# Gate tiles projected one ahead of the branch tiles, in an attention and mixture-of-experts step on one core

## The reference, cut to what matters

```python
g_da, g_mla, g_swa = jnp.split(jax.nn.sigmoid(h @ p['w_gate']), 3, axis=-1)
merged = (g_da * (o_da @ p['w_br_da']) + g_mla * (o_mla @ p['w_br_mla'])
          + g_swa * (o_swa @ p['w_br_swa']))
return merged @ p['w_o'], own
```

## Time and profile before

| | us |
|---|---|
| median of 3 runs | 3135.94 (3135.01 to 3138.71) |
| the profiled execution's own time | 3136.78 |
| its span | 3135.0 |
| PE busy | 2839.0 (91% of the span) |
| DVE busy | 2042.6 (65%) |
| ACT busy | 1637.1 (52%) |
| POOL busy | 237.0 (8%) |

### The profile page before, as it was taken

The page is one execution under the profiler, slowest core; times in us unless marked ns, Lnnn a source line. Parts: engine busy times, 40 slices in busy tenths (PEclk is TensorE's granted clock), DMA queues, the critical chain, the costliest instruction groups (busy, mean ns, idle before and its releaser), DMA issues.

```text
span 3135.0 us, 45603 instructions
## 1 busy us (share of the span) xinstructions
PE 2839.0 (91%) x16072; PEld 2248.9 (72%) x16072; DVE 2042.6 (65%) x3250; ACT 1637.1 (52%) x2385; POOL 237.0 (8%) x278
## 2 busy tenths in 40 slices
PE   6989988979979999999988898999799799999995
PEld 3868956968966777677657796588698577777774
DVE  3562355464358999999845424654634799999994
ACT  3262344243237777777634424432423577777774
POOL 0050012020000000000003200200200000000000
PEclk9999999999979999999999899999998799999997
DMA  7202100222369999999811021013033599999992
GB/s 285 87 2 90 58 29 28 82 70 76 120 225 329 338 338 338 337 337 333 299 70 61 28 93 55 1 62 116 28 121 129 195 340 336 332 337 338 333 350 73
DMA packets 280125, 564.15 MB, mean 180 GB/s; under 512 B 14040, under 2 KB 19872, under 8 KB 279328
## 3 DMA queue, kind: packets, MB, share of 16 engines
q1 hardware_dynamic: 273056, 543.25, 48.6%
q10 hardware_dynamic: 4448, 9.87, 0.9%
q0 software_dynamic: 2464, 8.91, 0.8%
HBM read 546.36 MB, written 15.63 MB: 179 GB/s over the span
## 4 chain that ended last, share of the span: by engine, by line
PE 65%; DVE 16%; ACT 7%; issue 6%; ACTq 2%; DVEq 1%; DMA 1%; POOL 0%; POOLq 0%; SPq 0%
PE mm L985 22%; PE mm L1461 19%; DVE w_lo L2024 7%; PE mm L998 6%; PE mm L1026 2%; DVE x L2032 2%; ACTq L1952 2%; ACT w_hi L1539 1%; PE mm L1213 1%; DVE scratch L2244 1%; ACT scratch L1539 1%; DVE scratch L2024 1%; ACT pt L1539 1%; PE mm L919 1%; PE oo L1313 1%
## 5 line engine op out<-in xcount | busy, mean ns | idle before, releaser
L2024 DVE TENSOR_TENSOR w_lo<-ring,w_hi 128x1024 fp32r<-128x1024 f32 x768 | 911.9, 1219 | 101.8 <-ACT w_hi L1539 85.5
L1539 ACT ACTIVATE w_hi<-ring 128x1024 fp32r<-128x1024 f32 x768 | 803.4, 1059 | 279.2 <-PE mm L1461 257.0
L2024 DVE TENSOR_TENSOR ring_lo<-ring,dw_hi 128x512 fp32r<-128x512 f32 x200 | 135.9, 683 | 400.7 <-ACT dw_hi L1539 399.8
L1539 ACT ACTIVATE dw_hi<-ring 128x512 fp32r<-128x512 f32 x200 | 124.0, 624 | 461.9 <-PE mm L985 456.2
L985 PE MATMUL mm<-h_hi,ring_lo 128*128 128x320 f32 (+1 forms) x1344 | 314.1, 315 | 15.9 <-DVE ring_lo L2024 13.4
L985 PE MATMUL mm<-h_lo,dw_hi 128*128 128x320 f32 (+1 forms) x1344 | 310.2, 312 | 0.0
L985 PE MATMUL mm<-h_hi,dw_hi 128*128 128x320 f32 (+1 forms) x1344 | 309.5, 312 | 0.0
L985 PEld LDWEIGHTS mm<-h_hi,ring_lo 128*128 128x128 f32 (+1 forms) x1344 | 225.3, 189 | 31.0 <-issue 29.0
L985 PEld LDWEIGHTS mm<-h_lo,dw_hi 128*128 128x128 f32 (+1 forms) x1344 | 226.6, 189 | 1.1
L985 PEld LDWEIGHTS mm<-h_hi,dw_hi 128*128 128x128 f32 (+1 forms) x1344 | 226.4, 189 | 1.1
L1461 PE MATMUL mm<-w_lo,xa_hi 128*80 128x512 f32 x512 | 204.9, 400 | 23.6 <-DVE w_lo L2024 11.8
(11 more groups left out here) (297 smaller groups left out, 5339.1 us busy)
## 6 DMA issues: line engine op xcount, KB each, us to landing
ring<-in_w_ff SPq DMA_DIRECT2D x384, 1024.0 KB, 6.4
ring<-in_w_ada SPq DMA_DIRECT2D x48, 1024.0 KB, 7.4
ring<-in_w_gate SPq DMA_DIRECT2D x24, 1024.0 KB, 5.7
ring<-in_w_in SPq DMA_DIRECT2D x16, 1024.0 KB, 9.0
ring<-in_w_o SPq DMA_DIRECT2D x8, 1024.0 KB, 8.2
x_spill<-x SPq DMA_DIRECT2D x2, 2560.0 KB, 13.2
ring<-in_w_br_da SPq DMA_DIRECT2D x4, 1024.0 KB, 5.0
ring<-in_w_br_mla SPq DMA_DIRECT2D x4, 1024.0 KB, 6.2
```

What stands on the lines that cost most here:

```text
L1539: return act.activation(out, in_, ACT.Copy, scale=scale)
L2024: return dve.tensor_tensor(out, in0, in1, op)
```

## The change

PE now computes gate tile m+1 before branch tile m. Gate tile 0 is cut in three pieces of 2, 2 and 4 steps (`first_gate`), put into the last three steps of each attention, behind the transposes of item s-2 or, in the last one, behind the last values. ACT and DVE make its hi and lo parts inside the attention: ACT two or three items before the end, DVE about one item later. For that the upper halves get their own buffers, `dw_da` in da's stage, `dw_tmp` (on the third `tmp` buffer and the one behind it) in the other two; the rope of sw's queries gives that place up and uses `sw_t`. The turns are renumbered: gate tile 0 and branch tiles 0 to 6 are in `mm[0]`, gate tiles 1 to 7 and branch tile 7 in `mm[1]`. In da's stage DVE's lo part of gate tile 1 is put into its normalisation steps.

```diff
+def gate_turn(turn, m):
+    return turn + (2 * m - 1 if m > 0 else 0)
+
+def branch_turn(turn, m):
+    return turn + (2 * m + 2 if m < KT - 1 else 2 * KT - 1)
...
+        dw_da = [rounded(f"dw_da{i}", "scratch", 8704 + i * HALF * P, [P, HALF, P]) for i in range(2)]
+        dw_tmp = [rounded(f"dw_tmp{i}", "tmp2", i * HALF * P, [P, HALF, P]) for i in range(2)]
...
+            def first_gate(l, g, q0, step):
+                if step == 0:
+                    wait_chunks(l, AT[l, "gate", g, 0], 2)
+                product_part(l, q0, (0, 2, 4)[step], (2, 4, 8)[step])
...
                 for m in range(KT):
-                    c = AT[l, "gate", g, m // 4]
-                    if m % 4 == 0:
-                        wait_chunks(l, c, 3)
-                    product_h(l, q0 + m)
+                    if m + 1 < KT:
+                        if (m + 1) % 4 == 0:
+                            wait_chunks(l, AT[l, "gate", g, 1], 2)
+                        product_h(l, q0 + m + 1)
                     if m == 0:
                         turned()
-                    product_branch(l, g, m, turn + 2 * m + 1, o_hi_, o_lo_)
+                    if m % 4 == 0:
+                        wait_chunks(l, AT[l, "gate", g, m // 4] + 2, 1)
+                    product_branch(l, g, m, branch_turn(turn, m), o_hi_, o_lo_)
...
+                    if s >= DA_N:
+                        first_gate(l, 0, H_AT["da_gate"], s - DA_N)
...
                 for s in range(DA_N + 2):
+                    if s == DA_N - 3:
+                        hi_of_tile(l, H_AT["da_gate"])
                     if s < DA_N:
                         da_exps(s)
                     if s >= 2:
                         turn_probs(l, TR["da"] + DA_TP[s - 2], s - 2, da_maps(s - 2)[1] // P)
-                wait_o_full(act, l, OO["da"] + DA_N - 1)
-                hi_of_tile(l, H_AT["da_gate"])
+                hi_of_tile(l, H_AT["da_gate"] + 1, (0,))
...
+                    if s == DA_N - 2:
+                        lo_of_tile(l, H_AT["da_gate"])
...
                     if s < SW_PAIRS:
                         sw_weights(s)
+                    if s == SW_PAIRS - 2:
+                        lo_of_tile(l, H_AT["sw_gate"])
                     if s >= 3:
                         sw_keep(s - 3)
```

More of the change, by code:

```diff
@@ L973, in product_h @@
                 out = h_out(j)
-                wait_mm_empty(pe, l, j)
-                for half in range(2):
+                if k0 == 0:
+                    wait_mm_empty(pe, l, j)
+                for k in range(k0, k1):
+                    half, kk = divmod(k, HALF)
                     u = 2 * q + half
-                    pe.wait_ge(dw_ready, l * 2 * H_N + (u + 1))
-                    for kk in range(HALF):
-                        k = half * HALF + kk
-                        if before is not None:
-                            before(k)
-                        w_hi_, w_lo_ = dw_hi[u % 2][:, kk, 0:width], chunk_lo(c + half)[:, kk, c0:c0 + width]
-                        for i, (w_, h_) in enumerate(((w_lo_, a_hi), (w_hi_, a_lo), (w_hi_, a_hi))):
-                            for lo, hi in HALVES:
-                                last = pe.matmul(out[0:width, lo:hi], w_, h_[:, k, lo:hi],
-                                                 start=(k == 0 and i == 0), stop=(k == KT - 1 and i == 2))
-                    last.then_inc(mm_full[j % 2] if half else dw_used, 1)
+                    if kk == 0:
+                        pe.wait_ge(dw_ready, l * 2 * H_N + (u + 1))
+                    if before is not None:
+                        before(k)
+                    w_hi_, w_lo_ = dw(q)[u % 2][:, kk, 0:width], chunk_lo(c + half)[:, kk, c0:c0 + width]
+                    for i, (w_, h_) in enumerate(((w_lo_, a_hi), (w_hi_, a_lo), (w_hi_, a_hi))):
+                        for lo, hi in HALVES:
+                            last = pe.matmul(out[0:width, lo:hi], w_, h_[:, k, lo:hi],
+                                             start=(k == 0 and i == 0), stop=(k == KT - 1 and i == 2))
+                    if kk == HALF - 1:
+                        last.then_inc(mm_full[j % 2] if half else dw_used, 1)
+            def product_h(l, q, before=None):
+                product_part(l, q, 0, KT, before)
+            def first_gate(l, g, q0, step):
+                if step == 0:
+                    wait_chunks(l, AT[l, "gate", g, 0], 2)
+                product_part(l, q0, (0, 2, 4)[step], (2, 4, 8)[step])
             def product_branch(l, g, m, j, o_hi_, o_lo_):
@@ L1566, in shifts, with hi_of_tile @@
                         .then_inc(h_ready, 1)
-            def hi_of_tile(l, q):
+            def hi_of_tile(l, q, halves=(0, 1)):
                 _, c, c0, width = h_tile(l, q)
-                for half in range(2):
+                for half in halves:
                     u = 2 * q + half
@@ L1611, in gates @@
                 for m in range(KT):
-                    j = turn + 2 * m
+                    j = gate_turn(turn, m)
+                    hi_of_tile(l, q0 + m + 1, first_halves if m == 0 else (0, 1))
+                    wait_mm_full(act, l, j)
+                    if m >= 2:
+                        wait_mm_read(act, l, branch_turn(turn, m - 2))
+                    act.activation(tmp[m % 2][:, :], h_out(j), ACT.Sigmoid).then_inc(mm_empty[j % 2], 1)
+                    if m == 0:
+                        turned()
                     for n in copied[m]:
@@ L1720, in _ @@
                 act.activation(da_r0, da_r0, ACT.Exp, scale=-0.5).then_inc(rs_done, 1)
-                gates(l, 0, MM["da_out"], lambda: [turn_out_da(t) for t in range(TT)], H_AT["da_gate"])
+                gates(l, 0, MM["da_out"], lambda: [turn_out_da(t) for t in range(TT)], H_AT["da_gate"], (1,))
                 act.wait_ge(merged_ready, l * 3 + 1)
@@ L2076, in rope, with lo_of_tile @@
                 return tt(dst, dst, t_[rows_, 0:NLAT], ALU.add)
-            def lo_of_tile(l, q):
+            def lo_of_tile(l, q, halves=(0, 1)):
                 _, c, c0, width = h_tile(l, q)
-                for half in range(2):
+                for half in halves:
                     u = 2 * q + half
@@ L2117, in lo_of_merged, with weigh, merge @@
                 tt(mg_lo[:, k, :], merged[:, k, :], mg_hi[:, k, :].bitcast(FP32), ALU.subtract).then_inc(mg_ready, 1)
-            def merge(l, g, turn, first, q0, turned=None, beside=None):
+            def weigh(l, turn, m, first):
+                t_ = tmp[m % 2]
+                wait_mm_read(dve, l, gate_turn(turn, m))
+                j = branch_turn(turn, m)
+                wait_mm_full(dve, l, j)
+                if first:
+                    tt(merged[:, m, :], h_out(j), t_[:, :], ALU.mult)
+                else:
+                    tt(t_[:, :], h_out(j), t_[:, :], ALU.mult)
+                    dve.drain()
+                    tt(merged[:, m, :], merged[:, m, :], t_[:, :], ALU.add)
+                dve.drain()
+                dve.sem_inc(mm_empty[j % 2], 1)
+            def merge(l, g, turn, first, q0, turned=None, beside=None, first_halves=(0, 1)):
                 _, _, _, kept = ada_plan(l, g)
@@ L2123, in merge @@
                 for m in range(KT):
-                    t_ = tmp[m % 2]
+                    lo_of_tile(l, q0 + m + 1, first_halves if m == 0 else (0, 1))
+                    if m == 0 and turned is not None:
+                        turned()
+                    if m >= 1:
+                        weigh(l, turn, m - 1, first)
                     for n in kept[m]:
```

95 lines of the change are left out of this document (47 added, 48 removed).

## The result

| | us |
|---|---|
| changed kernel, median of 4 runs | 3102.93 (3102.48 to 3104.18) |
| kernel before beside it, median of 4 | 3135.48 (3134.46 to 3138.71) |
| ratio | 0.9895, 95% interval 0.9878 to 0.9912 |
| the profiled execution's own time, its span | 3103.25, 3101.5 |
| PE busy | 2822.4 (before 2839.0) |

The change is faster by 33 us, 1.05%. The forecast was 3114, its range 3106 to 3126: the sign was right and the gain half as large again as the forecast, so the range missed the time. From profiled execution to profiled execution it is 33.5 us, where the sum had 21.8.

A forecast was written before the change was run, and what follows sets the result against it. PE was taken to bound the kernel, with gains only between an attention's end and branch tile 0. Da 5.0 and 3.7, mla 4.4 and 2.8, sw 0.9 and 0.7, output 4.3: 21.8 us off 3136.78, forecast 3114, range 3106 to 3126.

The forecast's parts named there:

- the sum: All six attention ends plus the transposed output: da 5.0 and 3.7, mla 4.4 and 2.8, sw 0.9 and 0.7, output 4.3.
- What bounds the kernel: Whole kernel: PE, busy 91% of the span, never stops inside gate and branch stages; gains lie only at the attentions' ends.
- The idle time: Attention's end to branch tile 0: PE's waits for last items, gate tile 0's parts and da's transposed output would shrink.
- the shift: Da's tail: ACT's hi copies and DVE's subtractions, now inside the attention, would delay PE by 0.8 us (0 to 2.4).
- The clock: Tails: low clock costs 1.7 us each in da and sw, none in mla; da's branch tile 0 left as slow.
- Rival B: Da and sw tails: clock stays up, saving 6.8 us and up to 2.3 twice in branch tile 0; 3108, chance 0.11.
- Sw: Sw's tail: 0.9 and 0.7 us won, after 1.3 for DVE's subtractions and 0.7 for POOL per layer.
- The 0.7 us for POOL: Sw's tail: POOL's scaling of item 18 and DVE's subtraction take the shared port in turn, 0.7 us per layer.
- The term for the transposed output: Da, gate tile to branch tile 0: the hole shrinks from 9.3 to 7.15 us, 2.15 won per layer.
- A: Tails: low clock lasts longer and all insertions are on the path, 10.1 us worse; 3124, chance 0.13.
- C: Tails: pieces cut off by waits never lift the clock, gate tile 0 and small groups at half speed; 3159, chance 0.04.
- D: Pieces wait for their parts, or holes only move behind gate tile 1; most of 21.8 us given back, 3134, chance 0.05.

The follow-up runs named there:

- the kernel with filled holes: Kernel before the change plus 32 and 25 matmuls per layer that compute nothing in da's holes, no order changed; ratio 0.9975, 7.8 us faster.
- the kernel of the run-ahead alone: Against the kernel before: gates one ahead of branches in all stages, gate tile 0 whole and its parts late; ratio 0.9980, 6.7 us won.
- the pieces alone: Against the kernel before: gate tile 0's parts early and the tile cut in all stages, tiles otherwise in old order; ratio 0.9980, 8.0 us won.
- the kernel with 20 matmuls more: The change plus 20 matmuls that compute nothing, once, in layer 1 before mla's attention; ratio 0.9901 to the kernel before.
- the kernel with the whole tile: The change with gate tile 0 uncut behind the last values, its parts still early; ratio 0.9936 to the kernel before, 3111.99 to 3119.75 us.

## Why the prediction was wrong, step by step

**What bounds the kernel: right.** The middle of the stages stayed without a stop, 115.00 of 115.00 us.

**The idle time: right in sum.** In da the trace has 6.0 and 4.9 us less. The prediction's terms give about 5.6 and 5.3, if the idle time before gate tile 0 in the old trace (4.3 and 3.9 us) goes, the hole shrinks by 2.15 and the shift takes 0.8. The hole behind gate tile 1 is 7.18 us in layer 0 (236.46 to 243.64) where the text had 7.15 (its terms, 0.55 and 6.55, make 7.10), and 6.72 in layer 1. The shift by the insertions was 0.5 us in da instead of 0.8: the transposes of item 18 start at 221.71 and 1733.46, which with the 0.20 and 16.85 us won ahead of the tails makes 221.91 and 1750.31, against 221.41 and 1749.82. In mla's layer 0 it was 4.4 us as predicted, and nothing was lost in the tail.

**The clock: the step that failed.** The prediction priced it at 1.7 us in each of da's tails and left branch tile 0 as slow as before. The sentences were "I take 1.7, since the pieces begin earlier" for da, and "The clock in branch tile 0 I leave as it is". In layer 0 no low stretch was paid for gate tile 0: from the transposes of item 18 (221.98) to its end (236.46 less 7.1 for gate tile 1) it took 7.4 us instead of 9.8. In layer 1 it took 9.8 as forecast, but branch tile 0 went from 6.4 us to 3.7, 2.7 us that the text had only as a bound of 2.3. Together with the shift and smaller small groups, da won 19.0 us instead of 13.0. The sum counted idle time taken out and let the clock's share stand; but idle time and low clock were in one hole, and the kernel with filled holes shows that 5.1 us per layer of it were clock alone. Some of layer 0's surplus was luck of the execution: its stage won 8.1 to 10.5 us in six traces, where 7.2 was forecast; layer 1's surplus of 3.2 us came in all three traces that can be compared. Rival B, at 0.11, had the right mechanism for da: it too took the low stretches as partly gone. It had it wrong for sw, where PE took the first piece at the lower level in both layers of the change (702.29 and 2215.64, 0.88 us for a pair that takes 0.54 at full clock). Its 3108 is still 5 us above the time.

**Sw: wrong in its parts.** DVE's pair does stand on the path (2.34 and 2.71 us of wait, before 1.77 and 1.65), 0.6 and 1.1 us more instead of 1.3. The 0.7 us for POOL was not paid: POOL's scaling took 1.60 us beside DVE's pair instead of 0.72, but the pair took its usual 1.27 and nobody waited for POOL. In layer 0 the whole gain was 3.3 in one trace and 0.7 in the other.

**Outside the stages: not foreseen.** The two traces have 3.5 us more that belong to no edited place, mainly 2.6 in mla's attention and 1.6 in sw's in layer 1. These are stretches of lower clock that, as far as one trace each can tell, come or go with the moment at which the attention begins. What decides which moments are good is open: 2.9 us later changed nothing, 0.9 and 1.7 us later did. The time left the range by both together. With da's surplus of 6.0 us alone it would have been 3108, inside it; the rest of the 11.7 us that the sum lacked came from mla's and sw's stretches.

**Which edit wins what: wrong, though the sum did not show it.** The text gave the pieces 17.5 us and the run-ahead 4.3. Alone they win 8.0 and 6.7. In da the pieces remove no idle time by themselves (0.2 and 0.1 us), since ACT and DVE set the start of branch tile 0, not PE; what the pieces free is used only because gate tile 1 then stands in the hole. The term for the transposed output (9.3 to 7.15) was right with and without the pieces: in the kernel of the run-ahead alone the hole is 6.73 and 7.15 us (244.35 to 251.08, 1767.75 to 1774.90). It is the 17.5 us that the pieces alone don't win.

**The rivals.** A (longer low clock, all insertions on the path; 3124) and C (slower; 3159) are refuted by the time and by the windows: the clock was back at 1.00 within the pieces, in layer 1 some 5.5 us after the first began. D is too: in mla and sw of the change PE goes from the last values to branch tile 0 without a stop, so no hole moved behind gate tile 1.

## What to carry to other kernels

A hole on TensorE costs its idle time and, in the traces here, up to half of the next 3 to 7 us of dense work behind it: price both from the windows, before and behind the edit. Two edits that shorten one chain must be priced together: where another engine's chain sets the end, the one that brings TensorE there earlier takes out no idle time until there is work to put in the hole. Gains of 2 to 4 us in places that an edit doesn't touch should not be counted as its own: in one trace a delay of 0.9 us elsewhere gave 3.0 us back. And trace the same instructions more than once: one stage's gain went from 8.1 to 10.5 us without an edit in it.

## What the runs showed of the hardware

- Work that computes nothing made the kernel faster. 114 matmuls of 320 columns in idle places of da's stage took the granted clock from 0.50 and 0.51 to 1.00 over gate tile 0 and gave 7.8 us.
- In layer 1 the clock's low stretches came back in both traces of the change: from 1660 us to 2440 they have the same eight, equally long and within 2 us of each other. In layer 0 they don't always: the traced execution of the kernel with 20 matmuls more lost 3.3 us in mla's attention there, ahead of its edit. The start matters too, in the one trace that tried it: 0.9 us of delay went with 3.1 us more of clock cost in two attentions behind it.
- Runs of one kernel can lie 8 us apart by the clock: of five runs of the kernel with the whole tile two took 3112 and 3114 us (mean clock 0.962 and 0.960), three 3119 to 3120 (0.957 and 0.958).
- Where DVE subtracts from two SBUF inputs, a GpSimd scaling beside it took 1.60 us instead of 0.72 and DVE's pair 1.27 as always; it was so in both layers (698.47 and 2211.82). The Trainium skill (SBUF — State Buffer, section on the two separate sides) gives the shared port to whichever of two such instructions starts first, for its whole length, and blocks the other. The trace agrees: DVE's pair began at 698.29 and lost nothing, the scaling began at 698.47 and paid.
